# Two layers with product-key experts on one core: the experts' softmax weights go through a grid in DRAM instead of one-hot matmuls

## The reference

```python
q = (xb @ w_q).reshape(T, PEER_HEADS, 2, PEER_HALF)          # 8 heads, 2 halves of 128
s = jnp.einsum('thpc,hpnc->thpn', q, keys)                   # 128 scores per half
sv, si = lax.top_k(s, PEER_TOPK)                             # 16 of 128, twice
cand = (sv[:, :, 0, :, None] + sv[:, :, 1, None, :]).reshape(T, PEER_HEADS, 256)
cv, ci = lax.top_k(cand, PEER_TOPK)                          # 16 of the 256 sums
e1 = jnp.take_along_axis(si[:, :, 0], ci // PEER_TOPK, axis=-1)
e2 = jnp.take_along_axis(si[:, :, 1], ci % PEER_TOPK, axis=-1)
eid = e1 * PEER_KEYS + e2                                    # one of 16384 experts
g = jax.nn.softmax(cv, axis=-1)
a = jnp.einsum('td,thkd->thk', xb, jnp.take(u_tab, eid, axis=0))
coef = g * jax.nn.gelu(a, approximate=False)
return jnp.einsum('thk,thkd->td', coef, jnp.take(v_tab, eid, axis=0))
```

## Time and profile before

| | |
|---|---|
| time, median of 3 runs | 3870.16 us (3866.17 to 3870.42) |
| time of the profiled execution | 3867.6 us |
| its span in the trace | 3865.9 us |
| TensorE busy | 3839.1 us (99%) |
| VectorE, ScalarE, GpSimd busy | 2532.3, 2065.4, 170.8 us |
| DMA queue of SP | 706.92 MB, 57.0% of 16 engines |
| DMA queue of GpSimd | 13.37 MB, 0.9% of 16 engines |

### The profile page before, as it was taken

The page is one execution under the profiler, slowest core; times in us unless marked ns, Lnnn a source line. Parts: engine busy times, 40 slices in busy tenths (PEclk is TensorE's granted clock), DMA queues, the critical chain, the costliest instruction groups (busy, mean ns, idle before and its releaser), DMA issues.

```text
span 3865.9 us, 58649 instructions
## 1 busy us (share of the span) xinstructions
PE 3839.1 (99%) x19628; PEld 3270.9 (85%) x19628; DVE 2532.3 (66%) x3843; ACT 2065.4 (53%) x3240; POOL 170.8 (4%) x150
## 2 busy tenths in 40 slices
PE   8999999999999999999999999999999999999999
PEld 8989988888888888888899889888888888888887
DVE  4565789878885555555564555889788875555555
ACT  5354444478885444444454544444688864444444
POOL 2110000000000000000121000000100000000000
PEclk9999999999999999999999999999999999999999
DMA  5455576655555666666454555666655556666665
GB/s 199 147 168 177 188 217 217 215 175 170 168 169 185 197 196 196 196 197 195 160 175 142 169 174 189 206 217 216 193 169 169 172 174 194 197 198 202 199 198 180
DMA packets 230743, 721.88 MB, mean 187 GB/s; under 512 B 29424, under 2 KB 58288, under 8 KB 230240
## 3 DMA queue, kind: packets, MB, share of 16 engines
q1 hardware_dynamic: 226640, 706.92, 57.0%
q0 software_dynamic: 3984, 13.37, 0.9%
HBM read 699.20 MB, written 6.29 MB: 182 GB/s over the span
## 4 chain that ended last, share of the span: by engine, by line
PE 96%; DVE 2%; DMA 1%; ACT 1%; issue 0%; DVEq 0%; SPq 0%; ACTq 0%
PE ps L2184 12%; PE ps L2185 12%; PE ps L2186 12%; PE ps L2108 12%; PE ps L2110 12%; PE ps L2109 12%; PE ps L1774 4%; PE ps L1775 4%; PE ps L1776 4%; PE ps L2161 2%; PE ps L1857 1%; PE ps L1859 1%; PE ps L1858 1%; PE ps L2122 1%; PE ps L2067 1%; DVE w_lo L1159 1%
## 5 line engine op out<-in xcount | busy, mean ns | idle before, releaser
L1159 DVE TENSOR_TENSOR w_lo<-w_raw,w_hi 128x1024 fp32r<-128x1024 f32 x1312 | 1633.4, 1246 | 1240.8 <-ACT w_hi L647 1210.1
L647 ACT ACTIVATE w_hi<-w_raw 128x1024 fp32r<-128x1024 f32 x1312 | 1389.8, 1061 | 1570.4 <-DMA w_raw<-in_v_tab 761.6
L2108 PE MATMUL ps<-w_hi,act_lo_t 128*128 128x512 f32 x2048 | 801.9, 392 | 1.1 <-DVE w_lo L1159 1.1
L2110 PE MATMUL ps<-w_hi,act_hi_t 128*128 128x512 f32 x2048 | 799.5, 390 | 0.0
L2184 PE MATMUL ps<-w_hi,act_lo_t 128*128 128x512 f32 x2048 | 797.9, 390 | 0.4 <-DVE w_lo L1159 0.3
L2186 PE MATMUL ps<-w_hi,act_hi_t 128*128 128x512 f32 x2048 | 796.9, 389 | 0.0
L2185 PE MATMUL ps<-w_lo,act_hi_t 128*128 128x512 f32 x2048 | 796.8, 389 | 0.0
L2109 PE MATMUL ps<-w_lo,act_hi_t 128*128 128x512 f32 x2048 | 796.6, 389 | 0.0
L2110 PEld LDWEIGHTS ps<-w_hi,act_hi_t 128*128 128x128 f32 x2048 | 384.2, 188 | 84.2
L2184 PEld LDWEIGHTS ps<-w_hi,act_lo_t 128*128 128x128 f32 x2048 | 384.4, 188 | 83.2 <-DVE w_lo L1159 1.9
L2186 PEld LDWEIGHTS ps<-w_hi,act_hi_t 128*128 128x128 f32 x2048 | 384.4, 188 | 80.0
(11 more groups left out here) (252 smaller groups left out, 2847.2 us busy)
## 6 DMA issues: line engine op xcount, KB each, us to landing
w_raw<-in_u SPq DMA_DIRECT2D x512, 512.0 KB, 3.5
w_raw<-in_v_tab SPq DMA_DIRECT2D x512, 512.0 KB, 3.7
w_raw<-in_dense SPq DMA_DIRECT2D x288, 512.0 KB, 3.5
big<-big SPq DMA_DIRECT2D x448, 32.0 KB, 3.0
x_spill<-big POOLq DMA_DIRECT2D x16, 256.0 KB, 4.6
big<-x_spill POOLq DMA_DIRECT2D x32, 128.0 KB, 4.0
big<-in_x_in SPq DMA_DIRECT2D x4, 512.0 KB, 5.1
big<-in_keys POOLq DMA_DIRECT2D x2, 1024.0 KB, 7.2
```

What stands on the lines that cost most here:

```text
L647: act.activation(w_hi[:, slot, :], w_raw[:, slot, :], ACT.Copy).then_inc(s_hi, 1)
L1159: dve.tensor_tensor(w_lo[:, slot, :], w_raw[:, slot, :], w_hi[:, slot, :].bitcast(F32), ALU.subtract).then_inc(s_lo, 1)
L2108: pe.matmul(o, act_lo_t[:, kb, t], w_hi[:, s % 4, c], start=kb == 0, stop=False)
L2110: ins = pe.matmul(o, act_hi_t[:, kb, t], w_hi[:, s % 4, c], start=False, stop=kb == KB - 1)
```

## The change

The one-hot matmuls go. The weights reach their places through an array in DRAM, `weight_grid`, with one float for each expert and token (16384 x 256, 16.8 MB).

- In the dense matmuls of each layer SP writes zeros over the grid: 32 transfers of 512 KB from `gb`, one after each 4 slab loads.
- Each search item computes its place in the grid itself: two more small VectorE instructions, which write `idx`.
- The softmax stays one over all 16 items. It is done at turn 16, slab 4, by VectorE's count, since VectorE splits the slabs of turn 16 in `quads_turn(15)`.
- GpSimd then issues 256 indirect transfers a layer. Each takes 128 weights (one of each partition) from a column of `cv` and adds them at the 128 places that a column of `idx` names. There are 16 for each item. Those of one half of the tokens wait until that half's previous item has landed.
- All turns but the last go through `turn_quads` and `shuffle`. The quads of turn 30 lie over `cv` and `idx`, so VectorE waits there until all transfers of the layer have landed.
- GpSimd then loads the grid back, 32 chunks of 512 KB, two at a time, and VectorE multiplies each into `big` (`weigh`) ahead of the blocks of the second table that read it.

```diff
+        grid = nc.dram_tensor("weight_grid", (N_KEYS * N_KEYS * T, 1), F32).ap()
-TOPK_STEPS = (4, 4, 2, 3, 3, 6, 1, 2)
+TOPK_STEPS = (4, 4, 2, 3, 3, 6, 1, 4)
...
+                sp.wait_ge(s_zero, layer + 1)
+                with sp.Fori(1, U_TURNS) as i:
+                    if layer == 0:
+                        dense_turn(i)
+                    else:
+                        dense_turn(i - 1)
+                    fill(i)
+                fill(0)
...
-                pool.wait_ge(s_slots, layer + 1)
-                pool.memset(at(K_TURNED + 2048, N_KEYS * T - K_TURNED - 2048), 1.0).then_inc(s_ones, 1)
...
+                for n in range(ITEMS):
+                    h, tb = n // TB, n % TB
+                    if n % PER_BATCH == 0:
+                        pool.wait_ge(s_slots, BATCHES * layer + n // PER_BATCH + 1)
+                    if h:
+                        pool.wait_ge(s_scattered[tb], 16 * TOPK * (HEADS * layer + h))
+                    for k in range(TOPK):
+                        pool.indirect_dma_start(grid, bass.IndirectOffsetOnAxis(ap=idx[:, n, k:k + 1], axis=0),
+                                                cv[:, n, k:k + 1], None,
+                                                compute_op=ALU.add).then_inc(s_scattered[tb], 16)
+                for tb in range(TB):
+                    pool.wait_ge(s_scattered[tb], 16 * TOPK * HEADS * (layer + 1))
+
+                def weights(c):
+                    if c >= 2:
+                        pool.wait_ge(s_weighted, U_TURNS * layer + c - 1)
+                    pool.dma_start(gb[:, c % 2, :].rearrange("p (q t) -> p q t", q=4),
+                                   grid_chunk(c).rearrange("(q p t) a -> p q (t a)", q=4, p=P)).then_inc(s_gb[c % 2], 16)
...
+                yield lambda: tk_chain(dve.scalar_tensor_tensor(out=expert, in0=e12[:, 0, :], scalar=float(N_KEYS),
+                                                                in1=e12[:, 1, :], op0=ALU.mult, op1=ALU.add))
+                yield lambda: tk_chain(dve.tensor_scalar(di, expert, float(T), tcol[:, tb:tb + 1], ALU.mult, ALU.add))
...
+                def weigh(c, b):
+                    if isinstance(c, int) and c == U_TURNS - 1:
+                        dve.wait_ge(s_mix, 2 * U_TURNS * (layer + 1))
+                    else:
+                        dve.wait_ge(s_shuffled[b], c * 128 + (256 * (SHUFFLES[b] * layer + 1) - 128 * b))
+                    dve.wait_ge(s_gb[b], c * 8 + (16 * (U_TURNS // 2 * layer + 1) - 8 * b))
...
+                    dve.tensor_tensor(rows, rows, gb[:, b, :].rearrange("p (q x f) -> p q x f", q=4, f=32),
+                                      ALU.mult).then_inc(s_weighted, 1)
...
                     dve.wait_ge(s_gelu, i * 2 + (2 * U_TURNS * layer + tb + 1))
+                    if tb == 0 and isinstance(i, int) and i == SHUFFLED - 1:
+                        for half in range(TB):
+                            dve.wait_ge(s_scattered[half], 16 * TOPK * HEADS * (layer + 1))
...
-                def scatter(i, s):
-                    done = SC_TURNS * layer
-                    if s % 2 == 0 and not (isinstance(i, int) and layer == 0 and 4 * (i - SC_FIRST) + s // 2 < 2):
-                        pe.wait_ge(s_sum, lin(i, 4, done * 4 + s // 2 - 1 - 4 * SC_FIRST))
-                    pe.wait_ge(s_hot2, lin(i, 8, done * 8 + s + 1 - 8 * SC_FIRST))
-                    pe.wait_ge(s_hot1, lin(i, 8, done * 8 + s + 1 - 8 * SC_FIRST))
-                    for x in range(2):
-                        ins = pe.matmul(ps[:, s % 4, T * x:T * (x + 1)], hot2[:, s % 2, x, :],
-                                        hot1[:, s % 2, x, :, :].rearrange("p c e -> p (c e)"), start=True, stop=True)
-                    ins.then_inc(s_hot_free, 1)
```

More of the change, by code:

```diff
@@ L364, in expert_block, with grid_chunk, quads_of @@
             return whole_turn(i * 2 + q // 4)[:, q % 4]
+        def grid_chunk(c):
+            n = 4 * P * T
+            rows = grid[c * n:(c + 1) * n] if isinstance(c, int) else grid[bass.ds(c * n, n)]
+            return rows
+        def quads_of(j, b):
+            return last_quads if isinstance(j, int) and j == SHUFFLED - 1 else turned_t[:, b]
         def xs(tb, c):
@@ L409, in _, with fill, dense_turn @@
                 n0 = SLAB0["qk", layer]
+                def fill(c):
+                    sp.dma_start(grid_chunk(c).rearrange("(p n) a -> p (n a)", p=P), gb[:, 0, :]).then_inc(s_filled, 16)
+                def dense_turn(i):
+                    for s in range(RING):
+                        load(s, i * RING + (n0 + s), dense[bass.ds(i * RING + s, 1)].rearrange("a p n -> (a p) n"))
                 if layer == 0:
@@ L435, in u_turn @@
                         u_load(i, s)
[L436 to L441, removed]
+                        exchange(i, b, s, ends, begins)
                 u_turn(0, 0, False, 0)
@@ L520, in _ @@
             pool.memset(credit[:, :], 0.0).then_inc(s_sc_ps, 1)
+            pool.memset(gb[:, 0, :], 0.0).then_inc(s_zero, 1)
+            step(pool.iota(tcol[:, :], pattern=[[32, TB]], base=0, channel_multiplier=1,
+                           allow_small_or_imprecise_dtypes=True))
+            step(pool.memset(above[:, :], 32.0))
+            step(pool.affine_select(out=above[:, :], in_=above[:, :], compare_op=ALU.is_ge, fill=0.0,
+                                    base=-32, pattern=[[-32, QUADS]], channel_multiplier=1))
+            for q in range(QUADS - 1):
+                step(pool.tensor_tensor(tcol[:, :], tcol[:, :], above[:, q:q + 1].broadcast_to([P, TB]), ALU.add))
             def whole(fill):
@@ L626, in _ @@
                         pool.dma_start(at(F_GAIN + w * g, w), last_gain[:, w * g:w * (g + 1)]).then_inc(s_last_gain, 16)
+                done = 0
+                for c in range(U_TURNS):
+                    weights(c)
+                    while c >= 2 and done < BACK and 2 * KB + RING + 12 * done + 6 < 8 * (c - 2) + 4:
+                        back(done)
+                        done += 1
+                assert done == BACK, done
+                if layer == 0:
+                    pool.wait_ge(s_weighted, U_TURNS)
+                    pool.memset(gb[:, 0, :], 0.0).then_inc(s_zero, 1)
                 if layer == 0:
@@ L1563, in topk_turn @@
+                    dve.transpose(quads_of(i, b)[:, tb, :], stage[:, :]).then_inc(s_mix, 1)
                 def topk_turn(item, n0, slabs, turn=None, b=None):
```

381 lines of the change are left out of this document (133 added, 248 removed).

## The result

The changed kernel takes 4275.74 us, median of 4 runs (4262.05 to 4282.89); the kernel before, run beside it, 3870.29 us. The ratio is 1.104 with a 95% interval of 1.101 to 1.107: **slower by 405 us**, where the forecast was 3779 us.

A forecast was written before the change was run, and what follows sets the result against it. TensorE's matmul order was taken as the bound. The profiled 3867.6 us, less 100 for one-hot work, plus 2 search, 6 reads and 1 first `weigh`, gave 3776.6; against the median, 3779 us, range 3765 to 4050.

The forecast's parts named there:

- the 6 us of the reads: Second table: 512 KB grid reads delay slab landings; 6 us for 64 reads, bounds 0 and 25 (0.4 us each).
- the 1 of the first `weigh`: Ahead of `c_lo`: the first `weigh` needs its grid chunk landed, +1 us.
- the 2 of the search: Search turns: VectorE's two further instructions for each item, 2 us, bounds 0 and 11.
- the gain of 100 us: First tables of both layers: one-hot matmuls and transposes leave TensorE's order, 50 us a layer, -100 us.
- the price of an indirect transfer: GpSimd, from turn 16: about 0.95 us each, between 0.56 and 1.34, so 256 end over 70 us early, cost 0.
- the limit of 1.24: Before turn 30's transposes: 317 us for 256 transfers, 1.24 us each; all hidden had chance 0.50.
- GpSimd too slow: VectorE's wait at turn 30: transfers only between splits, 1.36 us each (3840 us) or 2.72 (4537 us); chance 0.27.
- turning point of 1.42 us: Transfer price at which late transfers use up the 91 us gain; from there "GpSimd too slow" decides.
- The 2.0 us of the Trainium skill: Fixed time of a GpSimd transfer; if it held GpSimd each time, 512 us for 256, 4168 us in all.
- The engines flooded: DMA engines: each of a transfer's 128 pieces costs as much as a packet, 245 us late a layer, 4269 us; chance 0.08.
- 0 for the fills: Dense part: SP's 512 KB zero fills cost 0, bounds 0 and 25 us.
- The cover of 1.26 us a turn: Turns 0 to 13: VectorE's waits for ScalarE, 1.26 us a turn, cover the two search instructions' 0.4 us.

The follow-up runs named there:

- e10_bare: The changed kernel without indirect transfers or waits for them, filling one of the 32 grid chunks and reading two in each layer: 3792.6 us.
- e9_before_plus2: The kernel before, with two more small VectorE instructions for each searched item, their result unused: 3875.54 us against 3872.64, ratio 1.0008.

## Why the prediction was wrong

**The ledger.** The kernel after took 4275.7 us. Late transfers are 419 of them (less 3856.8 without any), the reads 46.5 and the fills 16.2. What stays, 3792.6 us, stands against 3770 in the forecast, its 3779 without the 6 us of the reads, the 1 of the first `weigh` and the 2 of the search.

**Of the gain of 100 us, 75 are seen** with nearly all of what comes taken out (3867.94 less 3792.6). In `e10_bare` the second table of layer 1 takes 698.0 us from its first to its last start, the slabs' own pace, and the one-hot matmuls are gone. The first matmul of its first and of its second table, layer 1:

```profile
L2099 PE MATMUL ps<-w_hi,act_lo_t x1024: 389/389/500, 2372.8 to 3080.9; 128*128 128x512 f32 x171
L2131 PE MATMUL ps<-w_hi,act_lo_t x1024: 387/389/504, 3081.9 to 3779.9; 128*128 128x512 f32 x171
```

The first table is 709.1 us in layer 1 (2372.8 to 3081.9) and 710.3 in layer 0, where 697.5 was forecast: 24 us short over both layers, which is the rest of 22 us in the ledger. Its waits in this kernel:

```profile
PE ps L2099 <- ACT stage L1085: 7.1, 10, 1.1
PE ps L2099 <- DVE w_lo L1187: 5.0, 14, 0.4
```

They are 12 of the 24 us: TensorE waits for the gelu, up to 1.1 us where I had one wait a layer, and for low parts in the turns of the search. The other half is in the same waits. Records of matmuls overlap by 0.16 us, so the idle time leaves out that much of each wait, and all of the shorter ones. From one start to the next, in the timeline, the starts that come over 0.03 us later than the usual 0.227 are late by 12.6 us in layer 0 and 11.2 in layer 1, each at line 2099 or right behind it.

All ten waits for the gelu follow a load of an activation table on ScalarE, which stands ahead of the first gelu in each pass of its loop over turns 16 to 30, three turns a pass:

```profile
859.57 1.28 ACT L1085 ACT_TABLE_LOAD   x1
860.87 0.60 ACT L1085 ACTIVATE stage<-ps 128x512 f32<-128x512 f32 x1
...
861.52 0.50 PE L2099 MATMUL ps<-w_hi,act_lo_t 128*128 128x512 f32 x1 [1.06 <-ACT stage L1085]
```

There are 12 such loads at the gelu in this kernel and 4 in the kernel before. Some 10 of the 24 us lie in these waits, the rest in those for low parts, of which `e9_before_plus2` puts a part down to the two search instructions. No run took the table loads away, so their share is read from the trace and not shown by an experiment.

**The step that failed** is the price of an indirect transfer. I wrote: "The lower bound is the cheapest issue on GpSimd, 0.56 us for line 536; the upper one from rows is 1.34 us for line 534", and took "the middle, about 0.95 us". Measured: 1.84 us at the least, 2.06 on average. The window and the count were right: 256 transfers in 317 us is 1.24 us each. (The window as a whole came later: the transfers started at 812.5 us, not 795, 10 us of it from the late start of the first table, and VectorE stood from 1140 and not 1116.6.) The upper end was the fault. A plain transfer's issue, however many pieces it has, doesn't bound an operation whose addresses GpSimd has to read and compute, and the text itself named that difference. With an honest upper end the chance that the limit of 1.24 holds could not have been 0.50.

**The rival that happened** is "GpSimd too slow", which had 0.27. Its place (VectorE's wait at turn 30) and its consequence (each us late is about a us, in both layers) hold. Its turning point of 1.42 us doesn't: without any transfer the kernel is only 13 us under the one before, so by an estimate the gain is used up at 1.24 + 13 / 512 = 1.27 us. Its mechanism is half right: a transfer isn't confined to the gaps between splits, only one that starts inside a split waits for its end. So the price lies between the rival's two: at 2.06 us its own rule gives 3779 + 512 x 0.82 = 4199 us. The rest to the result is the reads, the fills and the 24 us of the first tables. The rival worked with 1.36 or 2.72 us and had no case without any gap to wait for; the base price of 1.84 us makes 3779 + 512 x 0.60 = 4086 us by itself.

**The 2.0 us of the Trainium skill** (page "DMA: Bandwidth & Descriptors", section "Anatomy of one DMA — SWDGE (gpsimd) path"). The estimate from that figure, 4168 us, came nearer than my sum. That is luck: the price of 2.06 us is made of 1.54 on GpSimd, 0.30 to the next and the waits behind splits. I had set it aside because lines 534 to 536 are issued 1.2 us apart. That showed only that plain transfers don't hold GpSimd so long. The landing isn't what held it here either: the last transfer starts at 1337.17 us and VectorE goes on at 1340.46, so one takes about 3.3 us to land while the next starts after 1.84.

**The engines flooded** (0.08) is refuted. The DMA queues between 850 and 1050 us, kernel after (packets, MB, share of 16 engines):

```profile
q1 hardware_dynamic: 21800, 42.34, 75.1%
q0 software_dynamic: 13368, 0.05, 18.0%
```

The 94 transfers in this stretch are 142 packets each, about one for each piece, as that rival supposed, but a packet takes 0.18 x 16 x 200 / 13368 = 0.043 us of one engine and not 0.17. The slabs come in time but for some us (TensorE works 317.78 of 323), and half the transfers cost no more than that.

**Reads and fills.** I took 6 us for the reads with an upper bound of 25, and 0 for the fills. They were 46.5, beyond the bound, and 16.2. My bound of 0.4 us for each read came from the waits beside returns of 128 KB and wasn't scaled to 512 KB. The sum that took a slab beside a read from 3.7 to 5.3 us was too low as well: such slabs landed in 7.46 and 7.16. The mean share of the DMA (0.63 after against 0.60) was no guide: what counts is the one slab that is issued just behind the read. That the fills cost for the same reason is argued from the reads, not shown: in 128 KB pieces they still delayed the first table of layer 0.

**The search at +2, the first `weigh` at +1:** the first was some 3 to 4 us a layer in the traces of `e9_before_plus2`. The cover of 1.26 us a turn was an average over 19 waits of up to 3.0 us, and doesn't lie at every slab. The second can't be seen beside the rest.

## What to carry to other kernels

When a change puts a long queue of equal operations ahead of a fixed point, count and window give the price at which it turns; if the trace has no such operation, the nearest row of a simpler kind is a lower bound and not an upper one, and the chance has to say so. Work that one engine does in order should start as its inputs come, not when the last is there: the same 512 transfers cost 419 us from one starting point and none that can be told from eight. Background transfers are best cut to the slack of the loads beside them and spread: 512 KB in one piece cost a slab 3.8 us, and cutting all of them into four gave back 53 of 64 us, for the same bytes. When an engine is left without slack, its short waits count, and a profile's idle time shows only a part of them: the distance from start to start shows all.

## What was unexpected of the hardware

- An indirect transfer of 128 addresses with an addition holds GpSimd for 1.54 us, with 0.30 us before the next, whether VectorE is idle or reads one SBUF input; if it starts inside a split with two SBUF inputs it takes up to 1.17 us more, and the split stays at 1.23 us. In the kernel before, GpSimd's work of line 527 had stretched such a split to 2.22 us: there both sides lost (its own steps took 1.27 to 2.28 us), here one.
- From 1135 to 1341 us TensorE was busy for 8.49 us only, and its granted clock was 0.53, near the lower of its two levels (1.2 of 2.4 GHz); in the slices it is down to 5 in each hole and back at 9 in the one after. Behind TensorE's wait of 2.05 us at 1382.43 it was 0.58 over 3.8 us.
- A load of an activation table holds ScalarE for 1.28 us, and in `e10_bare` each of the ten ahead of the first gelu of a pass through three turns makes TensorE wait, up to 1.1 us.
